# SwiGLU gate and up products as seven half-width products for eight (Strassen), with weight sums and two elementwise products on GpSimd

## The reference, cut to what matters

```python
def swiglu(h, w_gate, w_up, w_down):
    return (jax.nn.silu(h @ w_gate) * (h @ w_up)) @ w_down

x = x + 0.5 * swiglu(rms_norm(x, g), w_gate, w_up, w_down)
```

## Time and profile before

| | |
|---|---|
| median of 3 executions | 3606.09 us |
| lowest, highest | 3604.7 us, 3608.92 us |
| span of the profiled execution | 3608.4 us |
| PE busy in the span | 3540.6 us, 98% |
| DVE, ACT, POOL busy | 57%, 43%, 9% |

### The profile page before, as it was taken

How to read it: one execution, slowest core, us unless ns; L and a number is a source line. 1 busy time by engine, 2 the same in 40 slices (tenths; PEclk the granted TensorE clock), 3 DMA queues, 4 the chain that set the end, 5 groups by cost and what they waited for, 6 DMA issues and landing times. The chain is left out here.

```text
span 3608.4 us, 49456 instructions
## 1 busy us (share of the span) xinstructions
PE 3540.6 (98%) x20379; PEld 2918.3 (81%) x20379; DVE 2041.9 (57%) x2881; ACT 1534.2 (43%) x2459; POOL 322.6 (9%) x307
## 2 busy tenths in 40 slices
PE   8999999999999999999999999999999999999998
PEld 6888788888788888887778778888988887877887
DVE  5987687775534454446686663444364744355743
ACT  5674678543423332222553432233353323275322
POOL 3772000000000000002111000000000000043000
PEclk9999999999999999999999999999999999999999
DMA  6345644333333333333320233333223333411332
GB/s 204 99 135 172 200 129 144 113 95 94 88 94 99 94 94 100 96 94 96 95 76 3 77 100 95 98 94 105 88 82 94 97 97 94 139 50 51 96 96 86
DMA packets 597624, 365.34 MB, mean 101 GB/s; under 512 B 16887, under 2 KB 578887, under 8 KB 596887
## 3 DMA queue, kind: packets, MB, share of 16 engines
q1 hardware_dynamic: 592807, 350.43, 32.8%
q10 hardware_dynamic: 4592, 11.73, 0.8%
HBM read 345.70 MB, written 15.89 MB: 100 GB/s over the span
## 5 line engine op out<-in xcount | busy, mean ns | idle before, releaser
L1377 PE MATMUL later_bank<-arena 128*128 128x512 f32 (+1 forms) x6792 | 1435.6, 373 | 9.8 <-DVE arena L1325 6.6
L1377 PEld LDWEIGHTS later_bank<-arena 128*128 128x128 f32 x6792 | 1193.2, 188 | 246.0 <-DVE arena L1325 14.3
L1317 ACT ACTIVATE arena<-arena 128x1024 fp32r<-128x1024 f32 (+3 forms) x545 | 566.4, 1039 | 1529.4 <-PE later_bank L1377 751.0
L1377 PE MATMUL middle_bank<-arena 128*128 128x512 f32 x4896 | 1125.5, 391 | 1.9 <-DVE arena L1325 1.1
L1377 PEld LDWEIGHTS middle_bank<-arena 128*128 128x128 f32 x4896 | 915.8, 187 | 210.4 <-issue 12.8
L1325 DVE TENSOR_TENSOR arena<-arena 128x1024 fp32r<-128x1024 f32 (+2 forms) x547 | 662.3, 1211 | 542.7 <-ACT arena L1317 537.0
L1377 PE MATMUL front_bank<-arena 128*128 128x512 f32 (+3 forms) x1776 | 349.4, 356 | 6.9 <-DVE arena L1325 4.7
L1377 PEld LDWEIGHTS front_bank<-arena 128*128 128x128 f32 (+1 forms) x1776 | 290.7, 188 | 62.9 <-DVE arena L1325 7.6
L1570 POOL TENSOR_TENSOR arena<-arena 128x512 f32<-128x512 f32 x120 | 171.2, 1426 | 113.3 <-ACT arena L1882 96.9
L1377 PE MATMUL ssd_bank<-arena 128*128 128x512 f32 x576 | 144.3, 402 | 0.2 <-DVE arena L1325 0.2
L2039 DVE SCALAR_TENSOR_TENSOR arena<-front_bank,columns,arena 128x510 f32<-128x510 f32 (+1 forms) x224 | 126.7, 628 | 18.1 <-ACT arena L1809 16.5
(11 more groups left out here) (486 smaller groups left out, 3014.0 us busy)
## 6 DMA issues: line engine op xcount, KB each, us to landing
arena<-in_w_in SPq DMA_DIRECT2D x114, 512.0 KB, 3.8
arena<-in_ffn_w_gate SPq DMA_DIRECT2D x76, 512.0 KB, 3.7
arena<-in_ffn_w_up SPq DMA_DIRECT2D x76, 512.0 KB, 3.7
arena<-in_w_mlp SPq DMA_DIRECT2D x64, 512.0 KB, 3.9
arena<-in_w_ada SPq DMA_DIRECT2D x48, 512.0 KB, 6.2
arena<-in_ffn_w_down SPq DMA_DIRECT2D x48, 512.0 KB, 4.0
arena<-scratch_cum SPq DMA_DIRECT2D x64, 256.0 KB, 6.7
arena<-in_gm_w_in SPq DMA_DIRECT2D x32, 512.0 KB, 3.8
```

Of the source, the lines that this page charges most:

```text
L1317: act.activation(self.high[q % self.AHEAD][:, 0:kb * cols], self.raw[self.slot(g)][:, 0:kb * cols], ACT.Copy).then_inc(self.high_done, 1)
L1377: ins = pe.matmul(out, still, moving, start=first and n_pass == 0, stop=last and n_pass == 2)
```

## The change

Gate and up are computed by Strassen's method in Winograd's form: an output pair (256 features) times two halves of 256 tokens, with the inner blocks taken in pairs, is made of seven products of 256 tokens where there were eight. Each job (`PairWork`) is one pair: two steps of 4x2 weight blocks (512 KB each, so loads now have rows of 256 features), 84 matmuls of 256 tokens for 48 of 512. There are 11 gate and 11 up pairs in each SwiGLU, in the order gate 0, up 0, gate 1, up 1 and so on. Down is cut into two jobs: the first 8 hidden blocks between gate 4 and up 4, the other 14 (in steps of 7 and 7) at the end; both add to the residual.

For each pair step GpSimd makes four sums of weights (three into one of four buffers, the fourth in place in the ring slot), ACT makes the high part of the slot and of the sums, DVE the two low parts. There are three high buffers for pair steps; `ahead(s)` is the last step whose high buffer is free once PE has done step s (s+3 for pair steps). The seven products lie in banks 0 to 6. ACT copies bank 0, and DVE adds the others in five operations (`combine`: 256, 512, 256, 256 and 512 wide). GpSimd then multiplies gate by the norm's factor, and silu by up. The operand of the pairs has seven combinations of blocks per two blocks of the residual (`PairHandoff`).

The core of the diff:

```diff
+class PairWork:
+    PARTS, PER, PRODUCTS = 2, 2, 7
...
+            if j.pair:
+                j.index, j.opens = pairs, held[0:j.PRODUCTS]
+                held[0:j.PRODUCTS] = [("first", pairs + 1)] + [("pair", 5 * pairs + n) for n in (1, 2, 4, 3, 5, 5)]
...
+    def take_high(self, used, count, g):
+        at = min(range(count), key=lambda b: used[b])
+        self.high_at.append(at)
+        self.high_after.append(used[at])
+        used[at] = g
...
+    def split_high(self, act, last):
+        while self.next_high <= min(last, len(self.split_steps) - 1):
...
+            self.wait_landed(act, g)
+            if self.high_after[q] >= 0:
+                act.wait_ge(self.products, self.unit_after[self.high_after[q] + 1])
...
+            act.wait_ge(self.summed, 4 * (r + 1))
+            act.activation(high, self.raw[self.slot(g)][:, 0:kb * cols], ACT.Copy)
...
+            act.activation(self.sums_high[r % len(self.sums_high)], self.sums[r % len(self.sums)], ACT.Copy).then_inc(self.high_done, 1)
...
+            rest = dve.tensor_tensor(low, raw, self.high[self.high_at[q]][:, 0:kb * cols].bitcast(F32), ALU.subtract)
+            if g in self.sums_index:
...
+                rest = dve.tensor_tensor(self.sums_low[at], self.sums[at], self.sums_high[r % len(self.sums_high)].bitcast(F32), ALU.subtract)
...
+    def ahead(self, s):
+
+        last = max((q for q in range(len(self.split_steps)) if self.high_after[q] <= s), default=0)
+        return next((q - 1 for q in range(len(self.split_steps)) if self.high_after[q] > s), last)
...
+    def sum_weights(self, pool, last):
+        while self.next_sum < len(self.sums_order) and self.sums_order[self.next_sum] <= last:
...
+            self.wait_landed(pool, g)
...
+            pool.tensor_tensor(s1, a21, a22, ALU.add).then_inc(self.summed, 1)
+            pool.tensor_tensor(s3, a11, a21, ALU.subtract).then_inc(self.summed, 1)
+            pool.wait_ge(self.summed, 4 * r + 2)
+            pool.tensor_tensor(s2, s1, a11, ALU.subtract).then_inc(self.summed, 1)
+            pool.wait_ge(self.summed, 4 * r + 3)
+            pool.tensor_tensor(a21, a12, s2, ALU.subtract).then_inc(self.summed, 1)
...
+    def copy_first(self, act, j, out):
...
+        act.wait_ge(self.pair_banks, 4 * j.index + 1)
+        act.activation(out[:, 2, :], self.banks[0][:, 0:TC], ACT.Copy).then_inc(self.emptied["first"], 1)
...
+    def combine(self, dve, j, out):
...
+        dve.wait_ge(self.emptied["first"], j.index + 1)
...
+        dve.tensor_tensor(sides, sides, self.all_banks[:, 5:7, 0:TC], ALU.add).then_inc(emptied, 1)
...
+    def pool(self, pool):
+        flow.sum_weights(pool, self.gates[0].step0 + 4)
+        for kind, p in self.products:
...
+            s = kind[p].step0
+            flow.sum_weights(pool, min(s + 5, self.jobs[-1].step0))
+            if kind is self.gates:
+                pool.wait_ge(self.into.ready, 1)
+                flow.wait_combined(pool, kind[p])
+                pool.tensor_tensor(whole, whole, rg.factor.unsqueeze(1).to_broadcast([P, 2, T]), ALU.mult).then_inc(self.hidden_by_pool, 1)
+            else:
+                flow.wait_combined(pool, kind[p])
+                pool.wait_ge(*self.silu_done(p))
+                pool.tensor_tensor(whole, whole, self.other, ALU.mult).then_inc(self.hidden_by_pool, 1)
+            flow.sum_weights(pool, min(s + 6, self.jobs[-1].step0))
...
     def scalar(self, act):
...
+            flow.copy_first(act, j, self.target(kind, p))
...
+            if silus:
+                silu()
+            if kind is self.gates:
+                silus.append(p)
+                flow.split_high(act, flow.ahead(j.step0 + 1))
+            else:
+                flow.split_high(act, flow.ahead(j.step0 + 1))
+                act.wait_ge(*self.multiplied(p))
+                act.activation(self.pair(p, self.high), self.pair(p, self.whole), ACT.Copy).then_inc(self.hidden_by_scalar, 1)
+            flow.split_high(act, min(flow.ahead(j.step0 + 2), self.next_pair(j)))
...
     def vector(self, dve):
...
+            flow.combine(dve, j, self.target(kind, p))
...
+                flow.split_low(dve, flow.ahead(j.step0 + 1))
+                dve.wait_ge(*self.high_done(p))
+                dve.tensor_tensor(self.pair(p, self.low), whole, self.pair(p, self.high).bitcast(F32), ALU.subtract).then_inc(self.hidden_by_vector, 1)
+            flow.split_low(dve, min(flow.ahead(j.step0 + 2), self.next_pair(j)))
...
+class PairHandoff(Handoff):
+    def round(self, act, k):
+        act.wait_ge(self.x_summed, 4 * (k + 1))
+        act.activation(self.x_high[:, k], self.x[:, k], ACT.Copy).then_inc(self.high_done, 1)
+    def rest(self, dve, k):
+        dve.wait_ge(self.high_done, 3 * (k + 1))
+        dve.tensor_tensor(self.x_low[:, k], self.x[:, k], self.x_high[:, k].bitcast(F32), ALU.subtract).then_inc(self.low_done, 1)
```

More of the change, by code:

```diff
@@ L2198, in __init__ @@
-        self.gate = Work(w_gate, [self.operand], (DB,), P, by="dve", ready=self.wait_operand)
-        self.up = Work(w_up, [self.operand], (DB,), P, by="dve")
-        self.down = Work(w_down, [lambda k: (self.high[:, k, :], self.low[:, k, :])], (8, 7, 7), P, by="dve",
-                        ready=lambda pe, k: pe.wait_ge(self.low_done, k + 1))
-        self.jobs = [self.gate, self.up, self.down]
-    def operand(self, k):
-        return self.into.parts(k)
-    def wait_operand(self, pe, k):
-        self.into.wait(pe, k)
+        arena, pairs = rg.arena, F2B // 2
@@ new lines, in __init__ @@
+        self.gates = [PairWork(w_gate, x, p, ready=None if p else lambda pe, k: self.into.wait(pe, k)) for p in range(pairs)]
+        self.ups = [PairWork(w_up, x, p) for p in range(pairs)]
+        first = 2 * self.FIRST_PAIRS
+        self.downs = [Work(w_down[at * P:(at + sum(cuts)) * P, :], [lambda k, at=at: (self.high[:, self.block(at + k), :], self.low[:, self.block(at + k), :])],
+                           cuts, P, by="dve", ready=lambda pe, k, at=at: pe.wait_ge(*self.low_done((at + k) // 2)))
+                      for at, cuts in ((0, (first,)), (first, (7, 7)))]
@@ new lines, in __init__, with silu_done, high_done @@
+        for j in self.downs:
+            j.banks = (7, *range(7))
+        self.down = self.downs[1]
+        self.products = []
+        for p in range(pairs):
+            ahead = p == self.FIRST_PAIRS
+            self.products += [(self.gates, p)] + [(self.downs, 0)] * ahead + [(self.ups, p)]
+        self.products.append((self.downs, 1))
+        self.jobs = [kind[p] for kind, p in self.products]
+    def silu_done(self, p):
+        return self.hidden_by_scalar, 2 * p + 1
+    def high_done(self, p):
+        return self.hidden_by_scalar, 2 * p + 2
@@ new lines, in add_down @@
+    def add_down(self, dve, order, j):
+        rg, resid, flow, before = self.rg, self.rg.core.resid, self.flow, self.into.before
+        first = j is not self.down
+        for s in range(j.steps):
+            for n in flow.blocks(j, s):
+                if first and before:
+                    order.then(dve.scalar_tensor_tensor(resid[:, n, :], resid[:, n, :], before.weight(n), before.first, ALU.mult, ALU.mult))
+                flow.wait_product(dve, j, n)
+                if n or not first:
+                    dve.wait_ge(self.resid_done, (0 if first else DB) + n)
+                dve.scalar_tensor_tensor(rg.scaled, flow.bank(j, n), 0.5, rg.factor, ALU.mult, ALU.mult).then_inc(flow.emptied["dve"], 1)
+                flow.wait_emptied(dve, j, n)
@@ L2281, in vector @@
                 dve.tensor_tensor(resid[:, n, :], resid[:, n, :], rg.scaled, ALU.add).then_inc(self.resid_done, 1)
[L2282 to L2283 removed]
+                if not first:
+                    self.out.vector(dve, n)
+            flow.split_low(dve, flow.ahead(j.step0 + s))
 class Gating:
```

401 lines of the change are left out of this document (284 added, 117 removed).

## The result

The changed kernel takes 3761.9 us (median of 4 runs, 3753.85 to 3765.08) where the kernel before takes 3605.39 us (3604.59 to 3608.92): 1.0427 of it, 95% interval 1.0414 to 1.044. It is 157 us slower; forecast were 86, and the time lies above the range.

The account below looks back on a forecast made before the run. TensorE's matmul stream was taken to bound the kernel before, and an in-order loop between up pairs after. Per SwiGLU -17.6 + 55.3 + 3.2 + 2.1 = +43.0 us, twice +86.0, gave 3692 us; range 3628 to 3750.

Parts of the forecast that it names:

- PE's gain: Gate and up pairs: 84 matmuls at 120.0 ns for 48 at 226.7 ns, 17.6 us less per SwiGLU, 35.2 in all.
- The loop: From up pair to up pair, queued work on GpSimd, ScalarE and VectorE takes 24.4 us a link, 26.3 with contention; nine links per SwiGLU.
- Contention: GpSimd and VectorE working together in the loop lengthen low parts and sums: 1.9 us more a link.
- The rival: The shared path into SBUF is the bound, without overlap: 27.9 us per gate and up pair, 3720 us; chance 0.2.
- The granted clock: In the pair jobs' stretches, a clock below 1.00 was expected nowhere; no cost was put in the sum.
- The edges: Start of a SwiGLU: parts of the larger operand stall PE's first half by 4.2 us, +3.2 against before.
- the last down job: End of a SwiGLU: a step more is free ahead, and it costs nothing.
- The first down job: The low part of its first step is queued behind gate 4's last adds: +2.1 us with the wait.
- The sum: Per SwiGLU -17.6 + 55.3 + 3.2 + 2.1 = +43.0 us, twice +86.0, giving 3692 us.
- The slower side: Whole kernel slower than before: chance 0.85, made of 0.48, 0.2 and 0.17.
- the bounds of the unknown durations: GpSimd's 256-wide times, load and contention taken low or high: links of 22.9 or 29.5 us, 3630 or 3750 us.
- The rival with the orders' loop not binding: Gate and up pairs: PE's columns set the time, with the chain under 21.5 us: 3581 us; chance 0.11.

Follow-up runs that it names:

- the fifth sum: Changed kernel with GpSimd making one more 128x256 sum of weights in each step: 3780.15 us, 18 us more than the changed kernel.
- the reordered copy: Changed kernel with the next pair's copy of bank 0 and adds ahead of the high and low parts of step s+5: 3696.11 us.
- with the clock held: Changed kernel with 38 unread matmuls of 256 columns at the start of each of the 18 up pairs that pause: 3728.27 us.
- changing the orders: Changed kernel with GpSimd's product before the sums of step s+5, and the next pair's copy and adds before that step's high and low parts: 3688.55 us.
- when all else was mended: Changed kernel with both orders changed and, at the edges, VectorE's low part made before the hand-over of rows: 3661.6 us.
- the edges give back 35.7 us alone: Changed kernel with only the low part made before the hand-over of rows (MLP, join, added down job): 3726.15 us.
- the run with both mended: Changed kernel with the low part made before the hand-over of rows and 38 extra matmuls in each of 18 up pairs: 3698.7 us.
- with every order, edge and product mended: Changed kernel with both orders and the edges changed, and both products (gate by factor, silu by up) back on VectorE: 3607.56 us.
- four versions of one loop: Links with both orders changed, 24.24 us; that with one more sum, 26.84; orders and edges changed with one product on VectorE, 22.62, or both, 21.52.
- with the product first: Changed kernel with only GpSimd's order changed, multiplying a pair before it sums step s+5: 3790.05 us.

## Why the prediction missed, step by step

- *PE's gain* (35.2 us): the price of a matmul was as forecast. 162 matmuls of 256 columns take 19.70 us at full clock, 121.6 ns each with their tail, for the 120.0 used.
- *The loop*: right in place, order and size. The nine pauses a SwiGLU end first with the copy and then with the add; PE goes on 16.7 us after the start for 16.9 forecast; the fifth sum adds 1.0 us a link; the reordered copy takes the loop down to 24.4 us; and with the clock held the link is 26.22 us for 26.3.
- *Contention*: the right size in the loop (sums of step s+5 4.7 us, as forecast). Not seen was how near the shared work is as a bound: 24.2 us a link, 2 below the loop. The rival priced it at 27.9 a link and 3720, with no overlap at all. The measured link of the changed kernel, 28.0, matches that by chance: without overlap, changing the orders could not have made the link shorter than 27.9, and it became 24.24.
- *The granted clock*: the step that failed. I wrote that I expected it below 1.00 nowhere, since pauses in the front of the trace had left it at its level. That row is a mean over slices of 90 us in tenths, and doesn't show a few us at half clock. The kernel before has such drops: one pause of 2.45 us ahead of its MLP, and short matmuls, are followed by 2.7 us at 0.59, as its own trace shows in a narrow window.

```profile
915.50 1.05 PE L2168 MATMUL middle_bank<-mean_of_width,arena 128*128 128x1 f32 x8 [2.45 <-DVE arena L2153]
918.76:921.44 2.68, 1.92 (x3) 0.37 (x3) 2.30 (x4) 1.38 (x2) 0.00 (x0) 0.59 0.00 0
```

  The drop after each pause costs 1.8 us a link (28.0 for 26.2 with the pauses filled), 33.6 us in all by the run with extra matmuls; the forecast had 0.
- *The edges*: the other step that failed. The hand-over itself was sized about right (a wait of 4.2 us forecast, 3.13 and 1.2 of clock when all else was mended); missing is what is queued behind it. I followed the new operand's parts up to the first gate pair, and not the low parts of the MLP's and the join's own steps, which stand behind them on VectorE. The prediction also said that the last down job costs nothing; the second SwiGLU's waits 0.97 us at each of six of its columns in the changed kernel, 0.29 before. In all the edges give back 35.7 us alone, 29.6 when the pauses are filled; why the two overlap by 6 us is not shown.
- *The first down job*: forecast +2.1 us, measured a wait of 1.98. Behind it the granted clock is below 1.00 as well, and the 192 matmuls take 45.4 us for 43.5, some 1.7 us beyond their tail that the forecast didn't have.
- *The sum*: 3692 + 63.2 (clock and edges, by the run with both mended) = 3755; 6.7 us of the 3761.9 have no cause shown.

The slower side (0.85) was right, and the range failed at its upper end, 3750, for one reason: it took in the bounds of the unknown durations, and neither of the two terms that stood at zero, the clock and the low parts behind the hand-over. The rival with the orders' loop not binding (3581) needed links under 21.5 us; even with every order, edge and product mended they were 21.52.

## What to carry to other kernels

A change that adds a pause to TensorE's stream also adds what the clock costs after it: read the granted clock in windows of a few us right behind pauses of that size, not in the page's row. Where an engine gets new work at a border between stages, list every instruction that stands behind it in its queue, also those of the stage that ends there, and not only the chain of the stage that begins. When GpSimd and VectorE both work in SBUF most of the time, add their work up, leaving out VectorE's instructions that read PSUM, and take some 0.85 of the sum as a bound of its own, beside the bound of each engine. The 0.85 is an estimate from four versions of one loop (25.6 to 30.8 us of such work).

## What the runs showed of the hardware

- The granted clock stays at 1.00 through a pause of 3.94 us and falls when TensorE starts again: 0.54 and 0.50 for 5.7 us, six matmuls in 1.42 us. A shorter pause can do it too, but its length doesn't tell. Behind the two waits of 2.10 us in the MLP of the changed kernel, both after a long run of matmuls, the first 3 us are at

```profile
1221.77:1224.77 3.00, 3.00 (x8) 2.42 (x9) 1.08 (x1) 0.00 (x0) 0.00 (x0) 0.61 0.35 106
1247.83:1250.83 3.00, 3.00 (x13) 2.46 (x14) 1.08 (x1) 0.00 (x0) 0.00 (x0) 1.00 0.29 86
```

  so 0.61 and 1.00. With the copy first, a pause of 2.08 us is followed by

```profile
1489.16:1495.00 5.84, 5.50 (x33) 5.25 (x34) 5.77 (x8) 3.33 (x4) 5.61 (x6) 0.71 0.20 69
```

  and with the product first, one of 1.68 us by 0.50 (1501.51 to 1504.50) and one of 2.21 us by 1.00 (1376.35 to 1379.35). With both orders changed, waits of 1.20, 1.35 and 0.76 us in each link leave it at 1.00. Matmuls that compute nothing, put into the pause, hold the clock: 684 of them made the kernel 33.6 us faster.
- A matmul has a fixed part of about 13 ns beyond its columns, at 512 as at 256 columns, so that 84 matmuls of 256 for 48 of 512 save 7% of the time and not 12.5%. The pair jobs at full clock confirm it, with 121.6 ns.
- GpSimd and VectorE beside each other, both with two operands in SBUF, do some 1.15 to 1.19 us of work in each us (27.9 in 24.24, 25.6 in 21.52). The Trainium skill (GPSIMD Engine Reference, "8. Key points") says that the two share interfaces to SBUF and contend when a VectorE instruction reads two inputs there; the trace agrees, with 1679 for 1225 ns on VectorE and 1435 ns for a GpSimd sum of 128x256 that takes 0.74 us with VectorE idle (at 1262.87 us in the changed kernel). Beside VectorE's adds from PSUM neither is longer: from 1358.19 us GpSimd's sums take 0.73 us, and the adds of 512 0.69 us, as alone.
